# Thirteen taps of a depthwise convolution between two tiles of a gated linear unit, counted on across channels' tiles, in place of eight within one

## The reference, cut to what matters

```python
h = rmsnorm(x, norm1_g[l])
z = h @ w_in[l] + b_in[l]
z_glu, z_rx, z_rg, z_ga, z_gb = jnp.split(z, split_idx, axis=-1)

u = z_glu[..., :D_CONV] * jax.nn.sigmoid(z_glu[..., D_CONV:])
u = causal_depthwise_conv(u, conv_dw_w[l], conv_dw_b[l])      # 31 taps, each channel by itself
u = jax.nn.silu(layernorm(u, conv_ln_g[l], conv_ln_b[l]))
y_a = u @ conv_w_out[l] + conv_b_out[l]
...
```

## Time and profile before

| | us |
|---|---|
| median of 3 runs | 2513.05 (2510.02 to 2513.66) |
| the profiled execution's own time | 2510.3 |
| its span | 2508.5 |
| TensorE busy | 2365.5 (94%) |
| VectorE busy | 948.3 (38%) |
| ScalarE busy | 929.6 (37%) |
| GpSimd busy | 1037.7 (41%) |

### The profile page before, as it was taken

How to read it: one execution, slowest core, us unless ns; L and a number is a source line. 1 busy time by engine, 2 the same in 40 slices (tenths; PEclk the granted TensorE clock), 3 DMA queues, 4 the chain that set the end, 5 groups by cost and what they waited for, 6 DMA issues and landing times.

```text
span 2508.5 us, 34111 instructions
## 1 busy us (share of the span) xinstructions
PE 2365.5 (94%) x10556; PEld 1922.4 (77%) x10556; DVE 948.3 (38%) x1601; ACT 929.6 (37%) x1628; POOL 1037.7 (41%) x796
## 2 busy tenths in 40 slices
PE   7999987899999998999997999998999997999997
PEld 6888866778888887888876777776666786888886
DVE  5699967435514214100114144444333343110012
ACT  4333374234322323333333533344333353443331
POOL 4455354444444443444453433332112254444443
PEclk9999998999999999999997999998899997999998
DMA  4334342437737432333331233333111331333331
GB/s 147 97 97 114 118 130 76 147 101 279 274 102 251 134 91 73 96 97 96 97 96 51 80 110 96 96 99 123 34 33 38 113 93 50 93 96 101 96 96 59
DMA packets 130557, 267.90 MB, mean 107 GB/s; under 512 B 14352, under 2 KB 14480, under 8 KB 129712
## 3 DMA queue, kind: packets, MB, share of 16 engines
q1 hardware_dynamic: 119520, 236.51, 31.4%
q10 hardware_dynamic: 10960, 30.38, 3.2%
HBM read 252.12 MB, written 14.68 MB: 106 GB/s over the span
## 4 chain that ended last, share of the span: by engine, by line
PE 82%; issue 7%; DVE 6%; POOL 3%; ACT 2%; DMA 0%; DVEq 0%; ACTq 0%; POOLq 0%
PE bank L851 24%; PE bank L853 23%; PE bank L852 23%; POOL wlo L374 2%; PE bank L1156 2%; PE bank L1188 1%; PE bank L1051 1%; PE bank L1053 1%; PE bank L1052 1%; PE bank L1102 1%; PE bank L1158 1%; PE bank L1170 1%; PE bank L1120 1%; DVE tmp L1507 1%; PE bank L961 1%
## 5 line engine op out<-in xcount | busy, mean ns | idle before, releaser
L374 POOL TENSOR_TENSOR wlo<-raw,whi 128x512 fp32r<-128x512 f32 x750 | 983.5, 1318 | 1365.9 <-ACT whi L446 1364.7
L851 PE MATMUL bank<-a_hi,whi 128*128 128x512 f32 x1992 | 797.0, 400 | 18.4 <-DVE a_lo L1261 7.1
L853 PE MATMUL bank<-a_lo,whi 128*128 128x512 f32 x1992 | 784.2, 394 | 0.0
L852 PE MATMUL bank<-a_hi,wlo 128*128 128x512 f32 x1992 | 784.0, 394 | 0.0
L446 ACT ACTIVATE whi<-raw 128x512 fp32r<-128x512 f32 x750 | 466.4, 627 | 776.6 <-PE bank L853 657.5
L851 PEld LDWEIGHTS bank<-a_hi,whi 128*128 128x128 f32 x1992 | 378.4, 190 | 113.6 <-issue 18.4
L853 PEld LDWEIGHTS bank<-a_lo,whi 128*128 128x128 f32 x1992 | 378.6, 190 | 80.8
L852 PEld LDWEIGHTS bank<-a_hi,wlo 128*128 128x128 f32 x1992 | 379.5, 191 | 74.5
L851 PE MATMUL bank<-b_hi,whi 128*128 128x512 f32 x788 | 316.5, 402 | 27.1 <-DVE G L1521 11.4
L852 PE MATMUL bank<-b_hi,wlo 128*128 128x512 f32 x788 | 312.1, 396 | 0.0
L853 PE MATMUL bank<-b_lo,whi 128*128 128x512 f32 x788 | 311.9, 396 | 0.0
(11 more groups left out here) (234 smaller groups left out, 1887.4 us busy)
## 6 DMA issues: line engine op xcount, KB each, us to landing
raw<-d_stream SPq DMA_DIRECT2D x750, 256.0 KB, 2.6
G<-d_ada SPq DMA_DIRECT2D x72, 512.0 KB, 4.6
spill_rv<-tmp ACTq DMA_DIRECT2D x32, 256.0 KB, 2.1
G<-spill_rv ACTq DMA_DIRECT2D x6, 1024.0 KB, 10.3
G<-d_x ACTq DMA_DIRECT2D x4, 512.0 KB, 5.4
spill_ga<-G ACTq DMA_DIRECT2D x8, 256.0 KB, 3.5
spill_gb<-G ACTq DMA_DIRECT2D x8, 256.0 KB, 3.5
G<-spill_ga ACTq DMA_DIRECT2D x1, 2048.0 KB, 8.1
```

Source lines behind the costliest of these rows:

```text
L374: pool.tensor_tensor(wlo[:, s % SRING, :], raw[:, s % RING, :], whi[:, s % SRING, :].bitcast(F32), ALU.subtract).then_inc(lo_done, 1)
L851: pe.matmul(out_ps, w_hi, hi[:, k, :], start=first and q == 0, stop=False)
L852: pe.matmul(out_ps, w_lo, hi[:, k, :], start=False, stop=False)
L853: mm = pe.matmul(out_ps, w_hi, lo[:, k, :], start=False, stop=last and q == len(ks) - 1)
```

## The change

The loop of two turns and the loop of six are written out as one straight piece. The gates stay eight, in the same order and on the same banks. The 248 taps are counted on across the channels' tiles: behind gate m follow taps 13 m to 13 m + 12 of the whole count, and behind the last gate all that are left. Tap x belongs to channels' tile x / 31. The instructions of a tap and of the add are the same; wait counts and addresses are constants.

```diff
-            with dve.Fori(0, 2) as i:
-                own.begin(i, TAPS)
-                for pr in range(4):
-                    j = pr % 2
-                    dve.wait_ge(evac[2 * j + 1], i * 2 + (pr // 2 + 2))
-                    dve.scalar_tensor_tensor(
-                        out=U[:, ds(i * 4 + (pr + 1), 1), PAD:U_ST].rearrange("p a t -> p (a t)"), in0=bank[2 * j][:, :],
-                        scalar=cols[:, ds(i * 8 + (COLS["b_in"][0] + 2 * pr), 1)], in1=R5[:, j, :],
-                        op0=ALU.add, op1=ALU.mult).then_inc(evac[2 * j], 1)
-                    dve.wait_ge(evac[2 * j], i * 2 + (pr // 2 + 2))
-                    conv_taps(i, 8 * pr, min(8 * pr + 8, TAPS))
-                own.end(2)
-            with dve.Fori(2, KD) as i:
-                own.begin(i - 2, TAPS)
-                conv_taps(i, 0, TAPS)
-                own.end(KD - 2)
+            for m in range(KD):
+                j = m % 2
+                dve.wait_ge(evac[2 * j + 1], m // 2 + 2)
+                dve.scalar_tensor_tensor(out=U[:, m + 1, PAD:U_ST], in0=bank[2 * j][:, :], scalar=col("b_in", 2 * m),
+                                         in1=R5[:, j, :], op0=ALU.add, op1=ALU.mult).then_inc(evac[2 * j], 1)
+                dve.wait_ge(evac[2 * j], m // 2 + 2)
+                for x in range(13 * m, 13 * m + 13 if m < KD - 1 else KD * TAPS):
+                    conv_tap(x // TAPS, x % TAPS)
```

More of the change, by code:

```diff
@@ L1407, in _ @@
             own.next(dve.tensor_scalar(lru_c[:, 1, :], w, 8.0, None, ALU.mult))
[L1409 to L1430, removed]
@@ L1445, in _, with conv_tap @@
-            with dve.Fori(2, KD) as i:
-                own.begin(i - 2, TAPS)
-                conv_taps(i, 0, TAPS)
-                own.end(KD - 2)
+            def conv_tap(m, k):
+                src, acc = U[:, m + 1, k:k + T], bank[6 + k % 2][:, :]
+                wk = col("conv_dw_w", 8 * k + m)
+                if k == 0:
+                    ins = dve.tensor_scalar(acc, src, wk, col("conv_dw_b", m), ALU.mult, ALU.add)
+                elif k == 1:
+                    ins = dve.tensor_scalar(acc, src, wk, None, ALU.mult)
+                else:
+                    ins = dve.scalar_tensor_tensor(out=tmp[:, 0, :] if k == TAPS - 2 else acc, in0=src, scalar=wk,
+                                                   in1=acc, op0=ALU.mult, op1=ALU.add)
+                own.behind(ins)
+                if k == TAPS - 1:
+                    own.all()
+                    dve.tensor_tensor(U[:, m, PAD:U_ST], bank[6][:, :], tmp[:, 0, :], ALU.add).then_inc(conv_done, 1)
+                    dve.wait_ge(conv_done, m + 1)
```

## The result

The changed kernel takes 2523.16 us (median of 5, 2521.54 to 2527.0) where the kernel before, measured beside it, takes 2513.05 (2508.79 to 2514.64): 10.1 us more by the medians. The ratio is 1.0049, with a 95% interval of 1.0037 to 1.0062, which is 9 to 16 us. Forecast were 2528, 2519 to 2535, and slower. Way and mechanism came as forecast; by the medians the size came out at two thirds of the 15.0 us forecast.

A forecast was written before the change was run, and what follows sets the result against it. TensorE, busy in every microsecond from 45 to 320 us, was taken to bound the touched stage. Pauses 11.0 plus clock 4.0 less 0 for the lead, +15.0 us on 2513.05, gave 2528, range 2519 to 2535.

The forecast's parts named there:

- The margin: Before the change, VectorE's second gate ended at 73.71 us and TensorE wanted bank 2 at 75.04: 1.3 us spare.
- the need of bank 2 at the third panel: TensorE waits for VectorE's second gate to free bank 2 before the third panel of the next turn.
- The pauses: Late second gates stop TensorE in four turns; losses of 2.2, 3.3, 3.3 and 2.1 us, 11.0 together.
- The clock: Behind the two longer pauses TensorE's clock falls, 2.0 us each, 4.0 in all; bounds 0 and 11.
- The lead: VectorE's convolution ends at about 244 us instead of 256.49, but no engine can use it: 0 us gained.
- The passing on of the delay: Behind 320 us ScalarE's last spill follows TensorE's last tile, so the delay is passed on whole.
- The sum: Pauses 11.0 plus clock 4.0 less 0 for the lead: +15.0 us, giving 2528.
- the first: Rival (a): the clock never falls, or once by little; 11 to 13 us, 2524 to 2526; chance 0.22.
- The rival of four falls: Rival (b): clock falls after three or four pauses, or as long as at 421.60; 2532 to 2535; chance 0.24.
- Faster taps in straight code: Rival (c): a tap comes down from 0.659 to 0.60 us; 2521 with no clock loss; chance 0.05.

The follow-up runs named there:

- the bank freed in another way: Thirteen taps behind each gate as in the changed kernel, but ScalarE copies the value out of PSUM and frees the banks: 2510.19 us, 0.9998 of the kernel before.
- the first profile: Profiled execution of the changed kernel in its first measurement against the kernel before: 2525.95 against 2510.3 us; median 2523.16 us.
- the second: Profile of the changed kernel measured again with no edit: 2524.31 us, ratio 1.0054 to the kernel before.
- the kernel of sixteen and ten: Changed kernel's 26 taps a turn, divided as 16 behind the first gate and 10 behind the second: 2538.06 us, 1.0121 of the kernel before.
- 8 and 18: Changed kernel's 26 taps a turn, divided as 8 behind the first gate and 18 behind the second: 2509.52 us, 1.0001 of the kernel before.

## Why the prediction was right, point by point

- **The margin** of 1.3 us and the need of bank 2 at the third panel: right. Four pauses at the four places named, and none behind; the bank freed in another way removes them.
- **The pauses**: forecast 2.0, 3.0, 3.0 and 1.9 us, measured 1.70, 2.61, 2.61 and 1.63. The mis-sized terms are the distances read from the loop code. The gate's first tap was put at 0.93 behind it; in straight code it is 0.79. In a turn with an end of a convolution the adding instruction starts 0.85 behind the last tap, not 0.91, and the next tap 0.04 after its end, not 0.18 (72.72 + 0.69 = 73.41, to 73.45). Two more terms were left out or misread. The first gate of a turn starts 0.10 behind the end of its sigmoid and not 0.27, which the prediction did not ask about; and the waiting matmul starts 0.13 us after the release, not the 0.05 read at one place of the earlier trace rows. For a plain turn that is 0.14 + 0.17 - 0.08 = 0.23 us, for one with an end 0.43, and these are the differences measured: 0.2 to 0.3, and 0.4. The loss with restarts was 9.6 us, not 11.0. The prediction took 0.18 instead of 0.31 for one idle time because no address has to be worked out any more, and left the others of the loop as they stood.
- **The clock**: forecast a fall at both longer pauses, 2.0 each, 4.0 in all. Measured one fall of 1.6 in the first profile and two of 1.5 and 1.6 in the second, all behind the pauses of 2.6 us and none behind those of 1.7. The step was right in kind and place; the price of a fall was a quarter too high. A pause of 3.7 to 4.6 us had one each time, at 1.9 on average.
- **The lead**: forecast worth nothing. Right, and shown by itself. Its size was put at 12 us (the convolution's end at 244); it was 17.5. The last gate came at 128.75 us and not at 132.6, by the shorter pauses and one fall of the clock for two; the taps behind it took 109.5 and not 110.5, since the ends of the convolutions cost less than the 1.18 us assumed. VectorE's new wait for the sum of the means was put at some 20 us and is 19.28.
- **The passing on of the delay** behind 320 us: right as far as the measurement tells. The 11.2 and 12.7 us of the stage are not taken up behind it: the medians say 10.1 and 14.3, and the profiles lag by 15.7 and 17.0 us at the end, for the parts that stay open above.
- **The sum**: forecast 15.0, of which 1.4 too much for the pauses and 0.9 to 2.4 for the clock; 11.2 and 12.7 at the end of the stage.
- Of the rivals, the first (little or no fall of the clock, 2524 to 2526) was nearest in size. The rival of four falls describes the kernel of sixteen and ten. Faster taps in straight code did not come: 0.66 us, as before. By the Trainium skill's page "TensorE: Matmul & The Clock Gate", section "HAM oscillation — how this bites in real kernels", a kernel that pauses anew each time pays the return anew; but the waits of the kernel in that section are some 3 to 5 us, and the prediction carried the rule over to shorter ones without saying so. The trace agrees where pauses were 3.7 to 4.6 us, each time, and in three of four cases at 2.6, and not where they were 1.7.
- The Trainium skill's page "VectorE: DVE Perf Modes", section "The DRAIN you can't avoid", says that a semaphore behind each instruction costs nothing extra. No run here shows that by itself, since every tap gives one in all these kernels. What the runs show is near to it: a tap's pace is 0.66 us with wait and register instructions of their own in the loop, and 0.66 without them.

## What to carry to other kernels

Before work is put ahead of an instruction of an engine with room, look for what that instruction frees, and when the bound engine wants it: the margin was 1.3 us here, two taps, although VectorE was idle for more than a third of the stretch. Work that has to be spread between releases goes behind the last release that is urgent, not evenly: the same 26 taps a turn cost nothing as 8 and 18, and 10 to 14 us as 13 and 13. A lead was worth something here only up to where its first user found its data ready.

## What the runs showed of the hardware

- A pause of TensorE has a price beyond its length that is not the same in each execution: behind pauses of 2.6 us the clock went to the 1.2 GHz level in three of four cases, for 1.5 to 1.6 us of loss each; behind pauses of 1.7 us in none of four; behind each of four pauses of 3.7 to 4.6 us, for 1.35 to 2.8 us.
- The wait and register instructions of a loop cost nothing between instructions that overlap (0.66 us a tap in both forms), but they do at a true dependence: 0.79 us against 0.93 from a gate to the tap that reads its result. Between the turns of a loop, where such a dependence meets the branch, 0.81 to 0.93 us of idle time became 0.04. Together that was 5.6 us of VectorE's time by the end of the convolution.
- A matmul that waited for VectorE to free its bank started 0.12 to 0.14 us after the freeing instruction's end at the four pauses of the changed kernel, and the matmul behind it 0.33 to 0.34 later instead of 0.227 (104.31 to 104.64, at the full clock).
